# Two transformer blocks on one core: which heads of the expert router add their gates to a table and which write them plainly

## The chip, the cores and the metric

One Trainium2 chip, one of its eight cores. The kernel is one program on that core. The metric is the device time of one execution in microseconds (us); runs of one kernel are compared by their median.

## The reference

The reference applies two blocks to 512 tokens of width 1024. The first mixes latent attention, a short convolution and attention to a memory; the second has two kinds of attention with 8 heads each. Both come before the part that matters here: the feed-forward part of the second block, a retrieval from 16384 experts of one neuron each.

```
q  = (xc @ wq).reshape(chunk, 8 heads, 2 halves, 128)
s  = einsum(q, subkeys)                      # 128 scores for each half
s1, i1 = top_k(s[half 0], 16);  s2, i2 = top_k(s[half 1], 16)
cs, ci = top_k(all 256 sums s1 + s2, 16)     # 16 picks for each token and head
eidx = i1 * 128 + i2 at the picks            # number of the expert, 0 to 16383
g  = softmax(cs)
hid = xc . u_table[eidx];   a = gelu(hid) * g
out = sum over heads and picks of a * v_table[eidx]
```

Each token has 8 x 16 = 128 picks. Two heads of one token may pick the same expert; its gate is then the sum of both. Within one head the 16 picks are different experts.

## The kernel before

**Gates as a dense table.** The kernel does not gather expert rows for the first 384 tokens (three blocks of 128, `DENSE = 3`). It multiplies those tokens with all 16384 experts and weighs every product with a gate that is zero for an expert that wasn't picked. The gates stand in a table in HBM, `gates`, of 128 tiles x 128 experts x 384 tokens, set to zero earlier by the SyncE queue. The fourth block of tokens is served by gathers of rows in the output stage.

**The stages from about 1050 us on.** First the queries are projected (unit "wq", 16 of them, line 1108) and scored against the sub-keys (line 1304); ScalarE copies the results (lines 1461 and 1637); GpSimd (POOL) makes the low halves of the split weights (line 950). Then TensorE transposes the residual (line 1314) and runs the hidden stage: 128 tiles, each of 128 experts against 512 tokens in 24 matmuls (line 1325). For a tile, SyncE loads the `u` weights into one of four slots (`load_u`), ScalarE makes their high part (`high_u`, line 1643), VectorE (DVE) their low part (`low_u`, line 1954), TensorE multiplies, ScalarE applies the activation (line 1378) into one of four slots, and for tiles 0 to 95 SyncE stores the result to HBM (`keep`). The activation of a tile waits until the store of the tile four before it has landed. In the last 32 tiles the results stay on chip. The output stage (line 1336) follows.

**The retrieval on VectorE** runs in the same time. `retrieve(h)` sorts one head in eight steps; between the steps stand calls of `low_u`, 8 of them in head 2 and 12 in each later head, in an order written out by hand (`FIRST_LOWS_AT`, `LOWS_AT`). `set_gates(h - 1)` stands after the fourth of the steps that step through head h (after the first for head 0's gates) and the `low_u` calls there; head 7's gates are set after four more `low_u`. Operations on one engine that depend on each other are chained by `link`, which makes VectorE wait for its own last instruction. VectorE's code is written out until 72 tiles are split, ScalarE's until tile 68; after that they loop. TensorE and SyncE loop from the fourth tile on.

**The scatters on POOL.** One scatter writes one pick of one head for the 128 tokens of a block: 128 elements of 4 bytes at indexed places in `gates`. There are 8 heads x 3 blocks x 16 picks = 384. Ten of them (head 0, block 0) stand between the weight splits of units 10 to 14; the others follow in the order of head, block, pick. At a head's first pick POOL waits for `s_tk`, which `set_gates` raises, and at the first pick in a block for the completion of all earlier scatters of that block. Heads 0 to 3 (`PLAIN = 4`) write plainly (line 980), heads 4 to 7 use the accumulating form of the scatter (line 983), which adds to what stands in the table.

**Equal picks.** A plain write replaces what an earlier head wrote. So for heads 1 to 3 VectorE adds to each new gate the gate that an earlier head gave the same expert: it compares the 16 new picks with the 16 h earlier ones (line 2056), multiplies with the earlier gates (line 2058), takes the maximum (line 2060; the latest gate of an expert holds the whole sum and is the largest) and adds it (line 2061). That is done for each of the three blocks.

**The end of the scatters** is waited for by SyncE, before it loads the first gates for the output stage, at tile 127 of the hidden stage.

Of the kernel before, what the change touches and what calls it, by code (L numbers as in the profile page):

```python
# [26 lines left out]
ALU = mybir.AluOpType  # L27
ACT = mybir.ActivationFunctionType
AX = mybir.AxisListType

P = 128
# [15 lines left out]
TOPK = 16  # L47
NT = 128
DENSE = 3
TD = DENSE * P  # L50
PLAIN = 4
LOWS_AT = (1, 2, 1, 2, 1, 2, 1, 2)
FIRST_LOWS_AT = (0, 0, 0, 1, 2, 2, 1, 2)
EARLY = 2
# [348 lines left out]
def program(nc, t_in, out):  # L403
    build_schedule()
    ctx = ExitStack()
    with ctx:
# [20 lines left out]
        def region(off, n, k=None, of=None):  # L427
            at, base = of or ((low, 0) if off < LOW else (blocks, LOW))
            v = at[:, off - base:off - base + n]
            return v if k is None else v.rearrange("p (k n) -> p k n", k=k)  # L430
# [18 lines left out]
        expert_gate = [region(o + 2 * P * tb + P, P) for tb in range(TB)]  # L449
# [5 lines left out]
        spare_off = o  # L455
# [52 lines left out]
        def rt(off, n, k=None):  # L508
            return region(TAIL + off, n, k, (tail, TAIL))
# [7 lines left out]
        eq = rt(15360, 1024)  # L517
# [16 lines left out]
        rated = rt(19984, P)  # L534
        token = rt(20112, 4)
        sum_before = rt(20116, TOPK)
        earlier = rt(20132, DENSE * TOPK * PLAIN, DENSE)
        gf = staged[:, 0:D]
        fss = staged[:, D:D + 16]
        fsq = staged[:, 2 * D:2 * D + 8 * T].rearrange("p (u n) -> p u n", u=8)  # L540
# [138 lines left out]
        sq0, n = {}, 0  # L679
# [12 lines left out]
        auxi, n = {}, 0  # L692
# [45 lines left out]
        for n, (kind, _, loads) in enumerate(PROJ):  # L738
            if kind in SPLIT:
                same = users[kind == "br"]  # L740
# [193 lines left out]
        def _(pool):  # L934
# [36 lines left out]
            def scatter(tb, k):  # L971

                h = k // TOPK
                if tb == 0 and k % TOPK == 0:
                    pool.wait_ge(s_tk, h + 1)
                if h and k % TOPK == 0:
                    pool.wait_ge(s_sc[tb], 16 * k)
                where = bass.IndirectOffsetOnAxis(ap=expert_no[tb][:, k:k + 1], axis=0)
                if h < PLAIN:
                    nc.gpsimd.indirect_dma_start(gate_elements, where, expert_gate[tb][:, k:k + 1], None)\  # L980
                        .then_inc(s_sc[tb], 16)
                else:
                    nc.gpsimd.indirect_dma_start(gate_elements, where, expert_gate[tb][:, k:k + 1], None,  # L983
                                                 compute_op=ALU.add).then_inc(s_sc[tb], 16)
# [3 lines left out]
            for s in STEPS:  # L988
# [14 lines left out]
                elif s[0] == "mem_squares":  # L1003
                    k, mm_, total = s[1], dtmp[:, MEM:2 * MEM], dtmp[:, 0:MEM]
# [723 lines left out]
        def _(dve):  # L1728
            V = nc.vector
            chain = [0]  # L1730

            def link(ins):

                chain[0] += 1
                ins.then_inc(s_d, 1)
                dve.wait_ge(s_d, chain[0])
# [242 lines left out]
            def retrieve(h):  # L1979

                for w in range(2):
                    yield from sorted_half(2 * h + w)
                    yield
                c4 = cand.rearrange("p (t a b) -> p t a b", t=TB, a=16)
                ch = cand.rearrange("p (t n) -> p t n", t=TB)
                shape = [P, TB, 16, 16]
                link(V.tensor_tensor(c4, tva[:, :, 2 * h, :].unsqueeze(3).to_broadcast(shape),
                                     tva[:, :, 2 * h + 1, :].unsqueeze(2).to_broadcast(shape), ALU.add))
                numbers = tif.rearrange("p (t w m) -> p t w m", t=TB, w=2)
                link(V.tensor_copy(numbers, tia[:, :, 2 * h:2 * h + 2, :]))  # L1990
                for tb in range(TB):
                    ins = V.max(cs[:, tb, 0:8], ch[:, tb, :])
                link(ins)
                yield
                for tb in range(TB):
                    ins = V.max_index(ci[:, tb, 0:8], cs[:, tb, 0:8], ch[:, tb, :])
                link(ins)
                for tb in range(TB):
                    ins = V.match_replace(ch[:, tb, :], cs[:, tb, 0:8], ch[:, tb, :], -BIG)
                link(ins)  # L2000
                yield
                for tb in range(TB):
                    ins = V.max(cs[:, tb, 8:16], ch[:, tb, :])
                link(ins)
                V.tensor_tensor(ee[:, h, :].rearrange("p (t k) -> p t k", t=TB), cs,
                                cs[:, :, 0:1].to_broadcast([P, TB, 16]), ALU.subtract).then_inc(s_sm, 1)
                for tb in range(TB):
                    ins = V.max_index(ci[:, tb, 8:16], cs[:, tb, 8:16], ch[:, tb, :])
                link(ins)
                yield  # L2010
                cif = ci.rearrange("p t k -> p (t k)")
                for w in range(2):
                    if w == 0:
                        link(V.tensor_scalar(ca, cif, 4, None, ALU.logical_shift_right))
                    else:
                        link(V.tensor_scalar(ca, cif, 15, None, ALU.bitwise_and))
                    link(V.tensor_copy(cbf[:, w, :], ca))
                    q3 = eq.rearrange("p (r m) -> p r m", m=16)
                    q4 = eq.rearrange("p (t k m) -> p t k m", t=TB, k=16)
                    link(V.tensor_tensor(q3, cbf[:, w, :].unsqueeze(2).to_broadcast([P, 64, 16]),  # L2020
                                         iota16.unsqueeze(1).to_broadcast([P, 64, 16]), ALU.is_equal))
                    link(V.tensor_tensor(q4, q4, numbers[:, :, w, :].unsqueeze(2).to_broadcast(shape), ALU.mult))
                    link(V.tensor_reduce(sel[:, w, :], q3, AX.X, ALU.add))
                    if w == 0:
                        yield
                number, place = cbf[:, 0, :], cbf[:, 1, :]
                ks = slice(TOPK * h, TOPK * (h + 1))
                link(V.scalar_tensor_tensor(number, sel[:, 0, :], float(NKEYS), sel[:, 1, :], ALU.mult, ALU.add))
                for tb in range(TB):
                    part = slice(TOPK * tb, TOPK * (tb + 1))  # L2030
                    ins = V.tensor_scalar(place[:, part], number[:, part], float(TD if tb < DENSE else P),
                                          token[:, tb % DENSE:tb % DENSE + 1], ALU.mult, ALU.add)
                link(ins)
                places = place[:, 0:TOPK * DENSE].rearrange("p (t k) -> p t k", t=DENSE)
                link(V.tensor_copy(expert_lists[:, 0:DENSE, ks].bitcast(U32), places))
                if h < PLAIN:
                    link(V.tensor_copy(earlier[:, :, ks], places))
                link(V.tensor_copy(row_no[:, ks], number[:, TOPK * DENSE:]))
                link(V.tensor_copy(hidden_no[:, ks], place[:, TOPK * DENSE:]))

            def set_gates(h):

                dve.wait_ge(s_ex, h + 1)
                e3 = ee[:, h, :].rearrange("p (t k) -> p t k", t=TB)
                link(V.tensor_reduce(es[:, 0:4], e3, AX.X, ALU.add))
                link(V.reciprocal(es[:, 4:8], es[:, 0:4]))
                ks = slice(TOPK * h, TOPK * (h + 1))
                ins = V.tensor_tensor(expert_lists[:, :, P + TOPK * h:P + TOPK * (h + 1)], e3,
                                      es[:, 4:8].unsqueeze(2).to_broadcast([P, TB, 16]), ALU.mult)
                if 1 <= h < PLAIN:  # L2050
                    n = TOPK * h
                    shape = [P, TOPK, n]
                    same = eq[:, 0:TOPK * n].rearrange("p (k m) -> p k m", k=TOPK)
                    for tb in range(DENSE):
                        link(ins)
                        link(V.tensor_tensor(same, earlier[:, tb, ks].unsqueeze(2).to_broadcast(shape),  # L2056
                                             earlier[:, tb, 0:n].unsqueeze(1).to_broadcast(shape), ALU.is_equal))
                        link(V.tensor_tensor(same, same, expert_gate[tb][:, 0:n].unsqueeze(1).to_broadcast(shape),  # L2058
                                             ALU.mult))
                        link(V.tensor_reduce(sum_before, same, AX.X, ALU.max))  # L2060
                        ins = V.tensor_tensor(expert_gate[tb][:, ks], expert_gate[tb][:, ks], sum_before, ALU.add)  # L2061
                ins.then_inc(s_tk, 1)

# [14 lines left out]
            for _ in range(4):  # L2078
                low_u(lows, lows % 4)
                lows += 1  # L2080
            set_gates(PEER_HEADS - 1)
            while lows % 4:
                low_u(lows, lows % 4)
# [185 lines left out]
```

## Time and profile before

| | |
|---|---|
| median of 3 runs | 2501.72 us (2491.94 to 2502.61) |
| the profiled execution, its own time | 2497.29 us |
| its span | 2495.5 us |
| granted TensorE clock, mean over the span | 0.961 |
| TensorE matmul busy | 2294.9 us, 92% |
| VectorE busy | 1299.1 us, 52% |
| ScalarE busy | 901.5 us, 36% |
| GpSimd busy | 1163.1 us, 47% |
| plain scatters, line 980 | 192, 198.4 us busy |
| accumulating scatters, line 983 | 192, 314.8 us busy |

The span is the time between the first and the last instruction that the profiler recorded; the execution's own time is 1.8 us longer. Busy time of the matmuls is modelled and they overlap, so a full PE in a window shows best by the number of its matmuls in that window. In the rows, PE is TensorE's matmul side, PEld its weight load, DVE is VectorE, ACT ScalarE, POOL GpSimd; "a<-b" names the output and inputs, `xN` counts instructions, and the clock is a share of 2.4 GHz. The queue q1 holds what SyncE issues, q0 what GpSimd issues.

### The profile page before, as it was taken

The page shows a single profiled execution, that of the slowest core. Times are in us where ns is not written, and L with a number is a line of the kernel's source. Part 1 is how long each engine was busy: PE and PEld are TensorE (multiplying, and loading weights), DVE is VectorE, ACT ScalarE, POOL GpSimd, SP SyncE. Part 2 cuts the span into 40 slices and gives each one's busy share as a digit, 9 for nine tenths or more (in the row PEclk, how much of TensorE's full clock was granted, in tenths as well). Part 3 has the DMA queues.
Part 4 walks back from the last instruction along what each step waited for, and adds up shares of the span by engine and source line. Part 5 has one row for each costly group of instructions (what it writes and reads, how often), then busy time and mean ns, then how long its engine had stood idle before and what let it go on. Part 6 is the DMA issues. An engine that isn't in the chain of part 4 may idle for free.

```text
span 2495.5 us, 29790 instructions
## 1 busy us (share of the span) xinstructions
PE 2294.9 (92%) x9705; PEld 1779.3 (71%) x9712; DVE 1299.1 (52%) x2403; ACT 901.5 (36%) x1419; POOL 1163.1 (47%) x817
## 2 busy tenths in 40 slices
PE   7999999999999998975596599999999999999998
PEld 5666566787766766764385488888888788888887
DVE  4355433136323563874374366622222488888887
ACT  3554543336434443312121133322222333333333
POOL 3332121244432213375454658888820366555554
PEclk9999999999999999987697799999999999999999
DMA  6554233325321112211242167666643699999997
GB/s 211 190 191 135 70 90 103 95 87 186 114 76 60 43 35 84 70 58 39 64 139 88 55 147 147 144 145 145 135 108 108 228 330 341 355 349 358 355 357 249
DMA packets 208210, 392.32 MB, mean 157 GB/s; under 512 B 56160, under 2 KB 131936, under 8 KB 207872
## 3 DMA queue, kind: packets, MB, share of 16 engines
q1 hardware_dynamic: 151296, 323.89, 39.9%
q0 software_dynamic: 56832, 67.45, 10.8%
q8 instruction: 38, 0.62, 0.1%
q14 instruction: 44, 0.36, 0.0%
HBM read 330.21 MB, written 61.01 MB: 157 GB/s over the span
## 4 chain that ended last, share of the span: by engine, by line
PE 52%; issue 4%; another core or an unknown queue 3%; DVE 1%; ACT 1%; POOL 0%; DMA 0%; DVEq 0%; ACTq 0%; POOLq 0%
PE bank L1325 26%; PE bank L1336 20%; PE bank L1108 5%; PE bank L1304 1%; ACT u_tiles_split L1643 0%; POOL low L1027 0%; PE bank L1314 0%; DMA tail<-hidden_of_last_block,low 0%; DVE low L1784 0%; ACT staged L1378 0%; DVE h_low L1806 0%; DVE tail L2058 0%; DVE tail L2056 0%; DVE tail L2060 0%
## 5 line engine op out<-in xcount | busy, mean ns | idle before, releaser
L1325 PE MATMUL bank<-h_high,u_tiles_split 128*128 128x512 f32 x2048 | 643.8, 394 | 70.5 <-issue 43.9
L950 POOL TENSOR_TENSOR u_split<-blocks,u_split 128x1024 fp32r<-128x1024 f32 (+1 forms) x115 | 283.0, 2461 | 700.0 <-ACT u_split L1471 668.9
L1108 PE MATMUL bank<-h_high,u_split 128*128 128x512 f32 (+1 forms) x1712 | 567.3, 406 | 22.4 <-DVE h_low L1806 17.8
L1336 PE MATMUL bank<-v_split,a_split 128*128 128x512 f32 x2286 | 520.3, 390 | 4.6 <-DVE a_split L2096 4.6
L1325 PEld LDWEIGHTS bank<-h_high,u_tiles_split 128*128 128x128 f32 x2048 | 390.2, 191 | 162.1 <-issue 79.3
L1336 PEld LDWEIGHTS bank<-v_split,a_split 128*128 128x128 f32 x2286 | 430.1, 188 | 94.9 <-DVE v_split L2093 5.4
L1325 PE MATMUL bank<-h_low,u_tiles_split 128*128 128x512 f32 x1024 | 403.7, 394 | 14.6 <-issue 14.4
L1954 DVE TENSOR_TENSOR u_tiles_split<-tail,u_tiles_split 128x1024 fp32r<-128x1024 f32 x128 | 156.6, 1226 | 487.6 <-ACT u_tiles_split L1643 448.4
L1108 PEld LDWEIGHTS bank<-h_high,u_split 128*128 128x128 f32 (+1 forms) x1712 | 324.6, 190 | 110.9 <-issue 23.1
L983 POOL DMA_INDIRECT gates<-low x192 | 314.8, 1640 | 87.2 <-issue 58.2
L1108 PE MATMUL bank<-h_low,u_split 128*128 128x512 f32 (+1 forms) x728 | 287.9, 395 | 0.0
L1027 POOL DMA_INDIRECT low<-in_v,low x128 | 140.2, 1095 | 296.6 <-DVE low L2112 143.6
L980 POOL DMA_INDIRECT gates<-low x192 | 198.4, 1034 | 148.2 <-DVE low L2061 91.5
L1677 ACT CAST v_split<-tail 128x1024 fp32r<-128x1024 f32 x128 | 134.9, 1054 | 300.9 <-PE bank L1336 227.1
L1325 PEld LDWEIGHTS bank<-h_low,u_tiles_split 128*128 128x128 f32 x1024 | 195.4, 191 | 55.7 <-issue 15.7
L1378 ACT ACTIVATE tail<-bank 128x512 f32<-128x512 f32 x96 | 57.4, 598 | 451.3 <-PE bank L1325 223.4
L2093 DVE TENSOR_TENSOR v_split<-tail,v_split 128x1024 fp32r<-128x1024 f32 x128 | 157.0, 1227 | 69.2 <-ACT v_split L1677 56.4
L1035 POOL DMA_INDIRECT tail<-hidden_of_last_block,low x128 | 167.9, 1312 | 43.5 <-issue 38.7
L2112 DVE SCALAR_TENSOR_TENSOR low<-low,tail 128x1024 f32<-128x1024 f32 x128 | 163.8, 1279 | 1.6 <-DMA low<-in_v,low 1.3
L1108 PEld LDWEIGHTS bank<-h_low,u_split 128*128 128x128 f32 (+1 forms) x728 | 138.2, 190 | 33.0 <-issue 6.4
L1643 ACT CAST u_tiles_split<-tail 128x1024 fp32r<-128x1024 f32 x128 | 133.1, 1041 | 8.0 <-DMA tail<-in_uT 6.5
L1856 DVE TENSOR_REDUCE low<-bank 128x1 f32<-128x512 f32 (+3 forms) x112 | 59.7, 535 | 143.1 <-PE bank L1239 71.5
(201 smaller groups left out, 2474.9 us busy)
## 6 DMA issues: line engine op xcount, KB each, us to landing
tail<-in_uT SPq DMA_DIRECT2D x128, 512.0 KB
tail<-in_v SPq DMA_DIRECT2D x128, 512.0 KB
gates<-blocks SPq DMA_DIRECT2D x32, 768.0 KB, 5.8
tail<-gates SPq DMA_DIRECT2D x128, 192.0 KB
kept_hidden<-tail SPq DMA_DIRECT2D x96, 192.0 KB
tail<-kept_hidden SPq DMA_DIRECT2D x96, 192.0 KB
blocks<-in_r SPq DMA_DIRECT2D x24, 512.0 KB, 4.0
blocks<-in_conv SPq DMA_DIRECT2D x16, 512.0 KB, 4.2
```

The costliest lines, as they stand in the source:

```text
L950: nc.gpsimd.tensor_tensor(flat(u, 1)[:, 0:n], ring[:, loads[0] % NW, 0:n], flat(u, 0)[:, 0:n].bitcast(F32), ALU.subtract).then_inc(s_wlo, 1)
L980: nc.gpsimd.indirect_dma_start(gate_elements, where, expert_gate[tb][:, k:k + 1], None)\
L983: nc.gpsimd.indirect_dma_start(gate_elements, where, expert_gate[tb][:, k:k + 1], None, compute_op=ALU.add).then_inc(s_sc[tb], 16)
L1027: nc.gpsimd.indirect_dma_start(rows_in[:, k % 4, :], None, v_rows, bass.IndirectOffsetOnAxis(ap=row_no[:, k:k + 1], axis=0))\
L1035: nc.gpsimd.indirect_dma_start(picked[:, k:k + 1], None, hidden_elements, bass.IndirectOffsetOnAxis(ap=hidden_no[:, k:k + 1], axis=0))\
L1108: last = mm(ps[0:m, :], flat(u, part)[:, k * m:(k + 1) * m], x, start=(k == 0 and j == 0), stop=(k == nk - 1 and j == 2))
L1325: last = mm(bank[slot % 2][:, :], U4[:, slot, w, k, :], x[:, k, :], start=(k == 0 and x is hh and w == 0), stop=(k == KD - 1 and w == 1))
L1336: done = mm(bank[2 + 2 * tb + dh][:, :], A2[:, slot, wa, tb * P:(tb + 1) * P], V2[slot // 2][:, slot % 2, wv, dh * T:(dh + 1) * T], start= ...
L1677: nc.scalar.copy(V2[slot // 2][:, slot % 2, 0], VR[:, slot, :]).then_inc(s_vhi, 1)
L1954: V.tensor_tensor(U4[:, slot, 1].rearrange("p k e -> p (k e)"), UR[:, slot, :], U4[:, slot, 0].rearrange("p k e -> p (k e)").bitcast(F32), ...
L2093: V.tensor_tensor(V2[slot // 2][:, slot % 2, 1], VR[:, slot, :], V2[slot // 2][:, slot % 2, 0].bitcast(F32), ALU.subtract).then_inc(s_vlo, 1)
L2112: V.scalar_tensor_tensor(sparse, rows_in[:, slot, :], rated[:, bass.ds(k, 1)], sparse, ALU.mult, ALU.add).then_inc(s_axpy, 1)
```

## The change

Heads 0 to 3 (`ADDED = 4`) now use the accumulating scatter into the zeroed table; heads 4 to 7 write plainly. Heads 0 to 3 no longer look for equal picks. Heads 4 to 7 do, in two parts. Against the 64 picks of heads 0 to 3 the gates of equal picks are summed, because each of those heads holds only its own gate. From head 5 on, the picks of the earlier plainly written heads are compared as well, with the maximum as before, and the larger of the two results is added. The list of earlier picks now holds all heads and moves to another free region of SBUF. The number of scatters, their order and their waits stay as they are.

```
-PLAIN = 4
+ADDED = 4
...
-        earlier = rt(20132, DENSE * TOPK * PLAIN, DENSE)
+        most_before = rt(20132, TOPK)
+        earlier = region(spare_off, DENSE * P, DENSE)
...
-                if h < PLAIN:
+                if h >= ADDED:
                     nc.gpsimd.indirect_dma_start(gate_elements, where, expert_gate[tb][:, k:k + 1], None)\
                         .then_inc(s_sc[tb], 16)
                 else:
...
-                if h < PLAIN:
-                    link(V.tensor_copy(earlier[:, :, ks], places))
+                link(V.tensor_copy(earlier[:, :, ks], places))
...
-                if 1 <= h < PLAIN:
-                    n = TOPK * h
-                    shape = [P, TOPK, n]
-                    same = eq[:, 0:TOPK * n].rearrange("p (k m) -> p k m", k=TOPK)
+                if h >= ADDED:
+                    n = TOPK * ADDED
+
+                    def equal_picks(tb, k0, k1, result, op):
+                        shape = [P, TOPK, k1 - k0]
+                        same = eq[:, 0:TOPK * (k1 - k0)].rearrange("p (k m) -> p k m", k=TOPK)
+                        link(V.tensor_tensor(same, earlier[:, tb, ks].unsqueeze(2).to_broadcast(shape),
+                                             earlier[:, tb, k0:k1].unsqueeze(1).to_broadcast(shape), ALU.is_equal))
+                        link(V.tensor_tensor(same, same, expert_gate[tb][:, k0:k1].unsqueeze(1).to_broadcast(shape),
+                                             ALU.mult))
+                        link(V.tensor_reduce(result, same, AX.X, op))
+
                     for tb in range(DENSE):
                         link(ins)
-                        link(V.tensor_tensor(same, earlier[:, tb, ks].unsqueeze(2).to_broadcast(shape),
-                                             earlier[:, tb, 0:n].unsqueeze(1).to_broadcast(shape), ALU.is_equal))
-                        link(V.tensor_tensor(same, same, expert_gate[tb][:, 0:n].unsqueeze(1).to_broadcast(shape),
-                                             ALU.mult))
-                        link(V.tensor_reduce(sum_before, same, AX.X, ALU.max))
+                        equal_picks(tb, 0, n, sum_before, ALU.add)
+                        if h > ADDED:
+                            equal_picks(tb, n, TOPK * h, most_before, ALU.max)
+                            link(V.tensor_tensor(sum_before, sum_before, most_before, ALU.max))
                         ins = V.tensor_tensor(expert_gate[tb][:, ks], expert_gate[tb][:, ks], sum_before, ALU.add)
```

## Rows read from the trace of the kernel before

**Rows 1.** The page's slices, 40 of 62.4 us; busy share in tenths.

```profile
PE   7999999999999998975596599999999999999998
...
POOL 3332121244432213375454658888820366555554
```

**Rows 2.** Windows: length, busy us (instructions) by engine PE to POOL, clock, DMA share, GB/s.

```profile
1500.00:1550.00 50.00, 50.00 (x222) 41.40 (x222) 30.99 (x86) 14.03 (x18) 42.37 (x26) 1.00 0.69 146
1181.35:1225.60 44.25, 12.28 (x25) 6.75 (x25) 1.23 (x1) 1.53 (x2) 29.69 (x31) 0.57 0.07 18
1308.73:1336.29 27.56, 6.10 (x12) 2.90 (x13) 0.00 (x0) 0.74 (x2) 18.84 (x20) 0.59 0.04 11
1389.00:1432.22 43.22, 14.28 (x43) 9.53 (x41) 9.08 (x43) 1.53 (x2) 29.03 (x30) 0.66 0.08 20
1156.00:1957.70 801.70, 717.74 (x3072) 585.17 (x3072) 337.65 (x812) 217.71 (x280) 464.69 (x336) 0.94 0.49 118
```

**Rows 3.** Timeline of POOL: start, duration, line, operation, idle time before it.

```profile
1094.88 0.99 POOL L980 DMA_INDIRECT gates<-low  x1 [0.17 <-issue]
...
1156.95 1.69 POOL L980 DMA_INDIRECT gates<-low  x1 [14.37 <-DVE low L2061]
...
1219.23 0.95 POOL L980 DMA_INDIRECT gates<-low  x1 [0.31 <-issue]
1267.67 1.69 POOL L980 DMA_INDIRECT gates<-low  x1 [47.49 <-DVE low L2061]
...
1332.40 0.96 POOL L980 DMA_INDIRECT gates<-low  x1 [0.31 <-issue]
1362.95 1.69 POOL L980 DMA_INDIRECT gates<-low  x1 [29.59 <-DVE low L2061]
```

**Rows 4.** Lines L980 and L983: duration ns min/median/max, first and last start.

```profile
L980 POOL DMA_INDIRECT gates<-low x192: 954/958/1940, 1063.1 to 1425.9; - x192
L983 POOL DMA_INDIRECT gates<-low x192: 1552/1559/2612, 1455.9 to 1827.4; - x192
```

**Rows 5.** Waits of ACT, 1140 to 1460 us: total, times, longest.

```profile
ACT tail L1378 <- remote: 130.4, 7, 35.1
```

**Rows 6.** DMA queues: 1308 to 1334 us above the dots, 1500 to 1550 us below.

```profile
q1 hardware_dynamic: 131, 0.47, 4.7%
q0 software_dynamic: 653, 0.01, 1.9%
...
q1 hardware_dynamic: 3947, 7.26, 48.0%
q0 software_dynamic: 3689, 0.01, 21.2%
```

**Rows 7.** Timeline of PE before and at the hidden stage's start.

```profile
1120.39 2.08 PE L1304 MATMUL bank<-tail 128*128 128x128 f32 x8 [16.15 <-issue]
1149.12 5.78 PE L1314 MATMUL bank<-low 128*128 128x128 f32 x32 [26.65 <-ACT staged L1637]
1156.06 0.50 PE L1325 MATMUL bank<-h_high,u_tiles_split 128*128 128x512 f32 x1 [1.16 <-ACT low L1663]
```

**Rows 8.** Timeline of DVE at the gates of heads 1, 2 and 3.

```profile
1151.97 0.43 DVE L2056 TENSOR_TENSOR tail<-tail 128x256 f32<-128x256 f32 x1
...
1260.29 0.69 DVE L2056 TENSOR_TENSOR tail<-tail 128x512 f32<-128x512 f32 x1
...
1352.44 0.21 DVE L2045 TENSOR_REDUCE tail<-tail 128x4 f32<-128x64 f32 x1
...
1353.16 0.96 DVE L2056 TENSOR_TENSOR tail<-tail 128x768 f32<-128x768 f32 x1
...
1356.14 0.17 DVE L2061 TENSOR_TENSOR low<-low,tail 128x16 f32<-128x16 f32 x1
...
1365.55 1.22 DVE L1954 TENSOR_TENSOR u_tiles_split<-tail,u_tiles_split 128x1024 fp32r<-128x1024 f32 x1
```

**Rows 9.** Timeline of PE, the matmul after that gap.

```profile
1366.83 0.50 PE L1325 MATMUL bank<-h_high,u_tiles_split 128*128 128x512 f32 x1 [0.81 <-DVE u_tiles_split L1954]
```

## The prediction, made before the changed kernel ran

> **What bounds the kernel now.** I read the page's slices first [rows 1]. TensorE is at 9 tenths nearly everywhere. The one long dip in the second half is in slices 17 to 22 (about 1060 to 1435 us), where PE falls to 5 tenths. It is where the gate table is written with plain scatters, so I went there.
>
> The windows table gives the rate of the hidden stage. Undisturbed it is 222 matmuls in 50 us [rows 2], 4.44 per us, so one expert tile (24 matmuls) takes 5.4 us. The whole stage has 3072 matmuls in 801.7 us [rows 2]; at the full rate they take 692. So 110 us are lost inside the stage. Three of its stretches hold nearly all: 25, 12 and 43 matmuls in 44.3, 27.6 and 43.2 us [rows 2], that is 80 where 511 would fit. PE runs there at 16% of its rate and 97 us are gone. The granted clock beside them is a mean of 0.57, 0.59 and 0.66 of 2.4 GHz, so near its lower level of 1.2 GHz most of the time; the other 12 us, 4 for each, go by my estimate in the return to the upper level after each stretch.
>
> What stands beside these stretches is POOL's stream of plain scatters [rows 3]. Streams start at 1156.95, 1267.67 and 1362.95 and end near 1220.2, 1333.4 and 1426.9 (the last one by the line's own row [rows 4]); PE starves 24, 41 and 26 us after each start and is back 3 to 5 us after each end. The later accumulating scatters run in one stream from 1455.9 to 1827.4 [rows 4], 192 of them at 1.945 us each, and windows in it are full. Meanwhile ScalarE waited 130 us, 7 times, for a transfer's completion ("remote") [rows 5], though in the starved stretch the load and store queue moved only 131 packets and the scatter queue took 1.9% of the DMA engines' time; with the accumulating form it takes 21.2%, and the load and store queue moves at 48% [rows 6]. So completions are late, not bandwidth short. The Trainium skill says (DMA: Bandwidth & Descriptors, "Queues, rings and completion order") that a DMA's semaphore increment lands only after every earlier write of that engine, across its queues; by that, late completions would follow the plain stream wherever it lies, which is the forecast's side. The same section has each engine take its queues in turn, which would keep a light stream from starving another; that is the first rival's side.
>
> A fourth stream begins at 1094.88 [rows 3] with head 0. PE is at the last key projections, waits 26.65 us for ScalarE's copy and starts its transposes at 1149.12, the hidden stage at 1156.06 [rows 7].
>
> **The change part by part.** Four sums, against the profiled execution (2497.3 us; the median of the runs shown is 2501.7, and 2497.3 is within them).
>
> A. Start of the hidden stage. Head 0 is now added. The ten early scatters sit between the weight splits; the accumulating form is 0.6 us longer (1559 against 958 ns [rows 4]), two in each of five projection units, 1.2 us a unit. The first units' idle time on POOL takes part of these 6 us and PE's lead over the last split the rest; I take 0, bounds 0 and 5. The other 38 no longer starve anything: PE was free for the last key scores at 1120.39 - 16.15 = 1104.2 [rows 7], so they end near 1105. The wait for ScalarE's copy shrinks to that copy, the transposes (5.8 us) run from 1106, and 1.2 later the hidden stage begins, near 1113, not 1156.06. Late next is the low part of the second tile on VectorE, by little. Gain 43 us, bounds 0 (it starves all the same) and 50.
>
> B. The three starved stretches, heads 1 to 3, go: 110 less the 0.8 of part C, gain 109. Bounds 0 and 109.
>
> C. VectorE. The comparisons of heads 1 to 3 (256, 512 and 768 elements) go, and cost PE 0.8 us; heads 5 to 7 do the same sizes among themselves. Added on top, for heads 4 to 7 and each of 3 blocks: three operations of 1024 elements and, from head 5, a maximum. Today head 3's block runs from 1352.44, the next tile's low part starts at 1365.55 [rows 8], a gap of 13.1 us, and PE waited 0.81 for it [rows 9]; so 12.3 us are covered by the tiles split ahead. A 1024-element operation takes 1.22 us, 1.26 with its gap; 768, 512 and 256 take 0.96, 0.69 and 0.43 [rows 8], with a gap of 0.03. A small operation takes 0.21 with its gap. The 0.7 us before and 2.9 after the comparisons stay.
> Head 4: 0.7 + 3 x (3 x 1.26 + 0.21) + 2.9 = 15.6, loss 3.3. Head 5 adds 3 x (3 x 0.46 + 0.21) = 4.8, loss 8.1. Head 6 adds 7.2, loss 10.5. Head 7 adds 9.5 but nothing follows it before the next split, 22.2, loss 9.9. Sum 32 us. Bounds: 10 (heads 6 and 7 fall in time that PE starves anyway) and 65 (VectorE has only about 65 us for a head, twelve tiles, and 31 of 50 us busy [rows 2] makes 40 of 65; plus 20 it is nearly full).
>
> D. The plain scatters' new place. POOL resumes adds near 1098; 182 of them at 1.945 take 354 us, to 1452. A head's gates are set after low part 26, 38, 50, 62 and 72 for heads 3 to 7 (the code's counts), when PE is at the third tile before: 1113 + 23 x 5.4 = 1237 for head 3, and with the block and the losses of C about 1315, 1387 and 1463 for heads 4 to 6. All are ready before POOL comes to them, so the plain stream starts at 1452 and runs through three heads: 144 scatters, the first 24 at about 1.4 us and the starved rest at 1.263 (the spacing in [rows 3]), 185 us, to 1637. PE starves from 30 us after the start (the mean of the three) to 4 after the end: 159 us, at 16% of its rate, 134 lost, and 4 for the clock. PE makes some 4.6 tiles in it, from tile 64 to 69, just where head 7's gates can be set; I let head 7 run by itself afterwards, losing what a stream of one head loses now, 109 / 3 = 36. D costs 174 us. Were head 7 in time, the stream is one of 242 us, and it costs 186. Lower bound 0 (no starving there; below it nothing is to be won, since nothing starves in that place now), upper 216, if PE stands still in all of a stream of 242 less 26.
> The stores that ScalarE waits for end at tile 96, which this stream doesn't reach. POOL ends near 1740, before PE ends the stage near 2011, and the load of gates waits for nothing new.
>
> The other edits (the moved list, one more small copy for each of heads 4 to 7, 0.2 us each) are within C. The output stage after 1958 is untouched: 0.
>
> Sum: 2497.3 - 43 - 109 + 32 + 174 = 2551 us.
>
> **The rivals.**
> 1. No starving late. Mechanism: what starves is not the plain form but the early place, where engines fetch fresh code (the 16.15 us before the last key scores are "issue" [rows 7]); decided at 1482, when the stream has run 30 us. Then D is 0: 2497.3 - 43 - 109 + 32 = 2377 us, much faster. For it: ScalarE and VectorE are in their loops by tile 68 and 72. Against it: PE and SyncE are in the same loops in the second and third stretch as later, and the adds from 1455.9 run beside the same unrolled code without a loss.
> 2. The starving is not continuous: each head costs about what it costs now, 36 us, four times 145. 2497.3 - 43 - 109 + 32 + 145 = 2522. For it: only streams of one head have been seen. Against: nothing in a stream lets up with time.
> 3. VectorE becomes the bound beside a fully starved stream: C 50 and D 205, 2600 us. For it: its budget in C; a stall of it also breaks up PE's clock.
> 4. The small writes starve whatever their form, so that adds beside the projections would as well. The skill (same page, "Specifications") has transfers under 512 B done by read-modify-write in either form. The long stream of adds in [rows 4] beside full windows speaks against that. A and B would be lost: 2497 + 32 + 174 = 2703, 2%.
>
> **How the numbers follow.** Forecast 0.52, rival 1 0.20, rival 2 0.16, rival 3 0.10, rival 4 0.02. The predicted time is the forecast's, 2551. The range must reach rivals 2 and 3 and some spread of theirs: 2465 to 2620, leaving out rival 1 (0.20) and rival 4. The forecast's own range, by bounds of A, C and D about it, is 2525 to 2590. This kernel's measurement tells 0.5% (12.5 us) from nothing. Faster: rival 1 and a thin edge of rival 2, 0.22. Within 0.5%: the rest of rival 2's lower half, 0.09. Slower: 0.69.
>
> **What would show it.** A: the first hidden matmul near 1113. B: full windows from 1113 to 1430. C: PE waiting for the split line of VectorE some 3, 8 and 10 us near heads 4 to 6. D: accumulating scatters from 1098 to 1452, then plain ones, and PE's windows at a fifth of their count from 1480 to 1640, with ScalarE waiting for "remote". If those windows hold 222 matmuls per 50 us, rival 1 is right and the prediction wrong; if PE starves between 1113 and 1430, rival 4 is.

## The result, and the profile after

The changed kernel takes 2573.11 us (median of 4 runs, 2566.92 to 2581.11), the kernel before on the same chip 2496.83 us (4 runs, 2487.37 to 2502.61). The ratio is 1.0311, interval 1.0263 to 1.0359: the change makes the kernel slower by about 76 us. The forecast was 2551. The profiled execution has a span of 2573.3 us, 77.8 above the span before.

The page's slices (40 of 64.3 us; PE and POOL in tenths of busy time, the granted clock, all DMA traffic in GB/s) answer to [rows 1]:

```profile
PE   7999999999899989999998861129999999999998
...
POOL 3431122245342213688888877750000265556664
PEclk9999999999999999999999985559999999999999
...
GB/s 210 187 191 126 72 94 106 91 115 180 71 86 50 42 41 91 91 99 143 144 134 121 120 74 13 12 24 149 143 109 107 174 332 333 354 352 359 349 354 257
```

The dip before (slices 17 to 22 of [rows 1]) is gone. A deeper one has come at slices 24 to 27, about 1480 to 1735 us, with POOL busy beside it. In slices 25 to 27 the clock is at its half and few bytes are moved.

The lines of the two scatters (duration min/median/max, first and last start; L984 is the accumulating form, L981 the plain one) answer to [rows 4]:

```profile
L984 POOL DMA_INDIRECT gates<-low x192: 1552/1556/2603, 1061.4 to 1457.4; - x192
...
L981 POOL DMA_INDIRECT gates<-low x192: 966/972/1970, 1460.0 to 1714.2; - x192
```

They change places at 1459, and both streams run without a gap. The windows of the changed kernel (length, busy time and instructions of PE, PEld, DVE, ACT, POOL, then clock, DMA share, GB/s) answer to [rows 2]:

```profile
1160.00:1210.00 50.00, 50.00 (x223) 41.40 (x222) 31.68 (x76) 16.83 (x21) 42.39 (x26) 1.00 0.67 147
1310.00:1360.00 50.00, 46.77 (x200) 38.16 (x199) 42.72 (x121) 15.93 (x21) 42.54 (x25) 0.97 0.62 127
1360.00:1410.00 50.00, 42.01 (x176) 34.31 (x175) 40.18 (x87) 11.54 (x15) 42.48 (x25) 0.90 0.56 115
1484.00:1531.00 47.00, 32.38 (x130) 23.33 (x128) 14.13 (x21) 9.21 (x12) 36.62 (x35) 0.94 0.26 77
1531.00:1728.00 197.00, 38.81 (x72) 21.03 (x72) 24.87 (x30) 4.85 (x8) 141.19 (x142) 0.52 0.06 12
1735.00:2035.00 300.00, 300.00 (x1325) 248.50 (x1324) 66.20 (x54) 85.39 (x111) 0.00 (x0) 1.00 0.42 129
1109.00:2035.30 926.30, 731.70 (x3072) 589.55 (x3072) 386.90 (x872) 216.56 (x279) 494.63 (x367) 0.88 0.41 103
```

In the columns of counts the first is PE's. Beside the adds its rate is the full one, 222 in 50 us; 200 and 176 are the windows with the searches of heads 4 and 5. From 1484 the rate falls, and from 1531 to 1728, 197 us, PE makes 72 matmuls where 875 would fit. After the stream it is at once full again for 300 us. The whole stage takes 926.3 us, 124.6 more than before, and begins at 1109.0, 47.1 earlier: together 77.5 us, the whole difference of the spans.

What PE and ScalarE waited for in the starved stretch (total, times, longest), as in [rows 5]:

```profile
PE bank L1326 <- issue: 155.3, 60, 21.2
PE bank L1326 <- ACT tail L1379: 17.6, 1, 17.6
```

```profile
ACT tail L1379 <- remote: 227.0, 7, 65.6
```

Again completions that don't come ("remote"), in waits of up to 65.6 us (before, 35.1). ScalarE's timeline shows that the work goes on in steps, one tile each time that such a wait ends:

```profile
1595.94 0.60 ACT L1379 ACTIVATE tail<-bank 128x512 f32<-128x512 f32 x1 [63.67 <-remote]
...
1663.09 0.60 ACT L1379 ACTIVATE tail<-bank 128x512 f32<-128x512 f32 x1 [65.61 <-remote]
...
1727.49 0.60 ACT L1379 ACTIVATE tail<-bank 128x512 f32<-128x512 f32 x1 [62.87 <-remote]
```

What is late is the completion and not the data. By the order of the slots, the activation at 1663.09 waits for the store that was issued at 1503.7, 159 us before; the bytes of that store, and of the next tile's stores and load after it, had all moved by 1518, and from 1518 to 1531 the load and store queue moved nothing. From 1610 to 1660 us again no load or store packet was moved, because nothing was left to move: the load issued at 1606.3 was through by 1610, and SyncE's next store was issued at 1663.9. The scatter queue took 1.8%:

```profile
DMA packets 1216, 0.02 MB, mean 0 GB/s; under 512 B 1216, under 2 KB 1216, under 8 KB 1216
...
q0 software_dynamic: 1216, 0.02, 1.8%
```

PE's own row has a second part. Most of its 60 waits for "issue" (nothing that the profile shows) are not between tiles but between single matmuls: within a tile most matmuls start 2.8 us after the one before, 2.2 of it idle, where the full rate is one in 0.225. The gaps between the tiles are 21.3, 21.2 and 17.6 us. What sets the 2.8 us no run shows. It is not what bounds the stretch: the tile activated at 1663.09 had been ready in PE's bank since about 1575.

The new waits on VectorE: PE's timeline at the searches of heads 4, 5 and 6.

```profile
1319.21 0.50 PE L1326 MATMUL bank<-h_high,u_tiles_split 128*128 128x512 f32 x1 [3.23 <-DVE u_tiles_split L1955]
...
1394.42 0.80 PE L1326 MATMUL bank<-h_high,u_tiles_split 128*128 128x512 f32 x1 [7.99 <-DVE u_tiles_split L1955]
...
1472.60 0.80 PE L1326 MATMUL bank<-h_high,u_tiles_split 128*128 128x512 f32 x1 [10.43 <-DVE u_tiles_split L1955]
```

### The profile page after: what moved, and what is told of

It is laid out like the page before. It is cut to its first block, busy times and chain, and to the rows that moved or that the text cites. A ratio compares the mean times of both kernels' runs of the same rounds, so it can differ in the third digit from the quotient of the medians.

```text
span 2573.3 us, 29842 instructions
## 1 busy us (share of the span) xinstructions
PE 2304.0 (90%) x9705; PEld 1779.7 (69%) x9712; DVE 1347.4 (52%) x2455; ACT 900.9 (35%) x1419; POOL 1182.3 (46%) x817
## 3 DMA queue, kind: packets, MB, share of 16 engines
q1 hardware_dynamic: 151296, 323.89, 38.5%
## 4 chain that ended last, share of the span: by engine, by line
PE 49%; another core or an unknown queue 8%; DVE 3%; ACT 1%; issue 1%; POOL 0%; DMA 0%; DVEq 0%; ACTq 0%; POOLq 0%
PE bank L1326 24%; PE bank L1337 20%; PE bank L1109 5%; DVE tail L2058 1%; DVE tail L2056 1%; DVE tail L2060 1%; PE bank L1305 1%; ACT u_tiles_split L1644 0%; DVE u_tiles_split L1955 0%; POOL low L1028 0%; DMA tail<-hidden_of_last_block,low 0%; DVE low L1785 0%; ACT staged L1379 0%; DVE h_low L1807 0%
## 5 line engine op out<-in xcount | busy, mean ns | idle before, releaser
L1326 PE MATMUL bank<-h_high,u_tiles_split 128*128 128x512 f32 x2048 | 652.7, 398 | 162.2 <-issue 121.7
L1028 POOL DMA_INDIRECT low<-in_v,low x128 | 149.2, 1166 | 479.6 <-PE bank L1326 321.3
L984 POOL DMA_INDIRECT gates<-low x192 | 327.7, 1707 | 57.6 <-issue 57.5
L981 POOL DMA_INDIRECT gates<-low x192 | 197.0, 1026 | 58.6 <-issue 58.6
```

What stands on the lines that cost most here:

```text
L1028: nc.gpsimd.indirect_dma_start(rows_in[:, k % 4, :], None, v_rows, bass.IndirectOffsetOnAxis(ap=row_no[:, k:k + 1], axis=0))\
L1326: last = mm(bank[slot % 2][:, :], U4[:, slot, w, k, :], x[:, k, :], start=(k == 0 and x is hh and w == 0), stop=(k == KD - 1 and w == 1))
```

## The experiments

The runs fell on four chips. On the first of them the kernel before took 2497.48 us (9 runs, 2489.96 to 2510.08), about as in the measurement above (whether that was the same chip isn't known); on the three others 2347.11, 2346.60 and 2346.53 (27, 13 and 13 runs, all between 2342.32 and 2351.97). This was not looked for, and it is the main finding beside the change's own effect. Each of the four chips was used only once, at another time than the others, so "chip" here stands for the chip with all that went with that one use of it. Each comparison below is with the kernel before on the same chip.

**First chip (kernel before 2497.48 us).**

**1. All heads added.**

```
-PLAIN = 4
+PLAIN = 0
```

> All 8 heads use the accumulating scatter and no head looks for equal picks (the sum needs none). Theory (the plain form starves the other engines): the hidden stage starts near 1110, runs full for 692 us to about 1802, and the scatters, 374 at 1.945 us from about 1098, end near 1826, so the last tiles' loads wait a little for them: 2573 - (2035 - 1826) = 2364 us, at best 2340. Rival (the place starves, from 1480 us on, whatever the form): starved windows stay between 1480 and the end of the scatters, 2550 us or more. Rival (accumulating scatters starve too when they stand first): no, since the changed kernel had full windows beside them from 1110 to 1310.

Measured: 2366.46 us (5 runs), ratio 0.9468, interval 0.9435 to 0.9500. The windows table of the whole hidden stage and the waits at its end:

```profile
1300.00:1350.00 50.00, 50.00 (x222) 41.42 (x221) 33.92 (x96) 16.63 (x21) 42.38 (x26) 1.00 0.67 144
1111.70:1808.00 696.30, 696.28 (x3072) 576.50 (x3072) 319.33 (x780) 216.43 (x279) 587.74 (x357) 1.00 0.66 136
```

```profile
PE bank L1335 <- DVE a_split L2093: 24.1, 1, 24.1
```

The stage takes 696.3 us, with no starvation anywhere, at a late place and beside unrolled code alike. The wait of 24.1 us at the change of stage is for the gates, whose last scatter starts at 1823.0. The place alone starves nothing, and the changed kernel starves in a late place: the rival that gave 2377 for the change is out.

**2. Plain scatters, slower.**

```
                 if h < PLAIN:
                     ...  # the plain scatter
+                    nc.gpsimd.memset(region(spare_off, 600), 0.0).then_inc(s_pace, 1)
+                    pace[0] += 1
+                    pool.wait_ge(s_pace, pace[0])
```

> The kernel before, with a 600-column fill of an unused region on POOL (and a wait for it) after each plain scatter, so that plain scatters come about every 1.9 us instead of 1.26, the spacing of the accumulating ones. Theory pace (completions starve because writes come too fast): no starved window, the hidden stage starts near 1113 and loses nothing: about 2497 - 152 = 2345, with the scatters' end near 1830 holding it up to 2365. Theory form (a plain scatter starves at any pace): a starved stretch becomes longer with the stream (48 x 1.9 = 91 us a head), about 60 us lost for each of heads 1 to 3 and for the start: 2560 us or more.

Measured: 2366.02 us (4 runs), ratio 0.9469, interval 0.9432 to 0.9507. The form is the same, 192 scatters of 964 ns (median); only the 0.61 us fill and its wait stand between them, so one starts 1.9 us after the other:

```profile
1200.63 1.02 POOL L982 DMA_INDIRECT gates<-low  x1 [0.28 <-POOL low L984]
1201.66 0.61 POOL L984 MEMSET low<- 128x600 f32 x1
1202.55 0.96 POOL L982 DMA_INDIRECT gates<-low  x1 [0.28 <-POOL low L984]
```

```profile
1300.00:1350.00 50.00, 50.00 (x222) 41.41 (x222) 35.20 (x94) 16.84 (x21) 42.95 (x52) 1.00 0.49 148
...
1108.20:1807.30 699.10, 696.83 (x3071) 576.55 (x3072) 346.01 (x817) 216.87 (x279) 592.74 (x534) 1.00 0.56 135
```

Full windows. So on this chip the plain form doesn't starve by itself; it does when one comes every 1.26 us, and not when one comes every 1.9 with POOL's fill and wait between (the pace and the pause were not tried apart).

**3. No search for equal picks.**

```
-                if h >= ADDED:
-                    ...  # the search and the sum
```

> The changed kernel without the comparison with earlier picks on any head, so a gate of an expert picked twice is wrong; the scatters stay as they are. The search costs TensorE what the trace shows as waits for VectorE near heads 4 to 6 (3.2, 8.0 and 10.4 us): the hidden stage is 22 us ahead when the plain stream begins, at the same time as before, so 2573 - 22 = 2551 us. If VectorE were a bound beyond these waits, 2530 or less. If the search is hidden, 2573.

Measured: 2566.87 us (4 runs, 2558.46 to 2567.41), ratio to the kernel before 1.0271, interval 1.0231 to 1.0311. That is 6 us less than the changed kernel's median, which was measured at another time, where 22 less were expected; the intervals of the two ratios overlap (1.0263 to 1.0359 for the changed kernel), so the 6 us are not clear of noise. The two profiled executions differ by 16.7. The trace shows where the rest of the gain went: PE comes to the stream further on, but the stream starts 9 us earlier (1450.9, where 1460.0 was the changed kernel's) and PE starves sooner. PE's windows around the stream, and what POOL waited for in it:

```profile
1440.00:1490.00 50.00, 33.80 (x136) 26.50 (x135) 20.33 (x44) 10.49 (x13) 39.03 (x37) 0.84 0.34 82
1490.00:1540.00 50.00, 7.04 (x12) 3.44 (x12) 0.00 (x0) 0.00 (x0) 38.11 (x40) 0.50 0.02 1
...
1590.00:1640.00 50.00, 9.34 (x18) 5.26 (x18) 1.23 (x1) 1.53 (x2) 35.41 (x36) 0.53 0.07 16
1640.00:1690.00 50.00, 35.12 (x125) 26.41 (x126) 6.66 (x8) 7.68 (x10) 21.71 (x22) 0.77 0.26 79
1690.00:1740.00 50.00, 22.62 (x61) 14.63 (x60) 4.20 (x4) 6.24 (x8) 25.81 (x27) 0.57 0.18 51
1740.00:1790.00 50.00, 50.00 (x222) 41.43 (x221) 11.73 (x10) 13.80 (x18) 0.00 (x0) 1.00 0.48 144
1108.70:2020.40 911.70, 732.70 (x3072) 589.82 (x3072) 319.17 (x780) 217.10 (x279) 478.32 (x366) 0.87 0.43 104
```

```profile
POOL gates L981 <- DVE low L2047: 25.8, 1, 25.8
```

PE has 12 matmuls from 1490 to 1540, where the changed kernel still had 130 from 1484 to 1531. So the low parts that head 7's gates stand behind came late, POOL waited 25.8 us for them and took up its stream at 1661.9, and head 7 then starved PE by itself. This is the course that the prediction had for the changed kernel. The price of the search under starvation isn't settled by this pair; experiments 7 and 8 measure it without starvation.

**4. Neighbouring places.**

```
-                    ins = V.tensor_scalar(place[:, part], number[:, part], float(TD if tb < DENSE else P),
+                    ins = V.tensor_scalar(place[:, part], number[:, part] if tb == DENSE else iota[:, ks],
+                                          float(TD if tb < DENSE else P),
```

> The kernel before, but the places of the dense blocks' gates come from the number of the pick and not from the expert: the 128 elements of one scatter lie side by side (512 bytes of one table row) instead of in 128 rows; the gates are wrong, the number, form, size and order of scatters are the same. If spread single-element writes in memory are what starves the others, the starved windows go: 2345 to 2365 us. If it is the scatter's form or pace whatever the addresses, 2497 us.

With this edit each scatter writes within one row of the table, and all scatters together within the rows of its first tile; the run doesn't tell these two kinds of crowding apart. Measured: 2676.64 us (4 runs), ratio 1.0712, interval 1.067 to 1.0755. Neither theory's number. The plain streams still starve the others ("remote"), and a second cost is there that the accumulating form has as well: PE's window beside it isn't full (143 matmuls in 50 us from 1550 to 1600), and ScalarE waits for the weights' loads, 304.6 of its 359.8 us between 1480 and 1880. ScalarE's waits, 1100 to 2100 us:

```profile
ACT u_tiles_split L1643 <- DMA tail<-in_uT: 359.8, 54, 15.1
...
ACT tail L1378 <- remote: 90.9, 4, 50.9
```

So the starvation does not need the 128 writes to be spread over 128 rows, and crowding them costs more than it saves.

**Second chip (kernel before 2347.11 us).** The next four kernels were made to find the limit of the pace. On this chip there was nothing to find it by.

**5 and 6. Shorter fills, 200 and 100 columns** in the diff of experiment 2.

> The kernel before with a 200-column fill after each plain scatter: about 1.5 us from one to the next (85 writes of 4 bytes per us; plain now 101, starving; accumulating 66, and plain behind the 600-column fill 67, both harmless). If the limit lies above 85 per us: no starvation, and the scatters end about 80 us earlier than with the long fill, so the wait of 24 us at the change of stage goes too: 2366 - 24 = 2342 us. If it lies below, completions pile up more slowly than now, a part of the starvation stays: 2380 to 2480 us.

> The same with a 100-column fill: about 1.4 us, 91 writes per us. Limit above 91: 2342 us. Between 85 and 91: more than the 200-column kernel, 2400 us or more. If it is not a matter of pace but of whether POOL does anything else between two scatters, both fills give the same as the long one but end earlier, 2342 us.

Measured: 2347.19 us (11 runs), ratio 1.0004, interval 0.9995 to 1.0014; and 2345.47 us (10 runs), 0.9995, interval 0.9983 to 1.0007. The first expectation's 2342 is nearly met, but the kernel before has the same time here, so this tells nothing of the limit. Both were run once more on other chips:

> The kernel before with the 100-column fill (one plain scatter in about 1.38 us, 93 writes per us). Beside a kernel before of 2497 us: if the limit lies above that pace 2345, if below, a part of the starvation: 2380 to 2490. Beside 2347: 2347 again, which tells nothing of the limit.

> The kernel before with the 200-column fill (one plain scatter in about 1.5 us). Beside a kernel before of 2497 us: 2345 if the limit of pace lies above 85 writes per us, 2380 to 2480 if below it. Beside 2347: 2347 again.

Measured: 2344.90 beside 2346.60 (ratio 0.9996, interval 0.9985 to 1.0007), and 2347.95 beside 2346.53 (1.0002, 0.9989 to 1.0015). Again chips without starvation. What the repeats do show is that the fills cost nothing there: POOL has the time.

**7. The changed kernel, plain scatters with the long fill.** The diff of experiment 2 in the changed kernel, for `h >= ADDED` (the fill stands in another unused region).

> The changed kernel with the 600-column fill after each plain scatter (now heads 4 to 7). Theory pace: nothing starves in the late place either; what is left of the change is the search on VectorE, now for all four heads at full speed, 3.2 + 8.0 + 10.4 + 10 = 32 us: hidden stage 1109 + 692 + 32 = 1833 us, past the scatters' end near 1823, so 2573 - (2035 - 1833) = 2371 us. If the late place had a cost of its own: 2420 us or more.

Measured: 2385.58 us (4 runs), ratio 1.0171, interval 1.0155 to 1.0187, that is 38.5 us above the kernel before on this chip. This is the price of the search, with nothing starving. The expected 2371 was 14.6 too low. The hidden stage takes 737.2 us where 724 were worked out. PE's four waits for VectorE are 31.9, as foreseen; but without any starvation or such waits the stage takes not 692 us but 696.3 (experiment 1), and about 9 us are lost beside the waits. The granted clock falls there: it is a mean of 0.90 in the window with head 5's wait in the changed kernel of the result.

**Half the elements in a plain scatter** (`expert_no[tb][0:64, k:k + 1]` and the gates likewise).

> The kernel before, but a plain scatter writes only 64 of the 128 tokens of its block (the other tokens' gates of heads 0 to 3 are left out). Number of scatters and of semaphore increments as before. If the number of written elements per us starves (64 in at most 1.26 us is 51 per us or, should a scatter take half the time, up to 100): with the instruction as long as before no starvation, 2342 to 2350 us; if it becomes half as long, 2450 or more. If scatters or their increments per us do it: 2497 us or more.

Measured: 2348.91 us (10 runs), ratio 1.0013, interval 1.0003 to 1.0023. Inconclusive for the same reason. It shows one thing: a scatter of 64 elements takes POOL 892 ns (median), one of 128 takes 958 (median, kernel before), so POOL's time for one hardly depends on the number of elements.

**Third chip (kernel before 2346.60 us). 8. The changed kernel once more.**

> The changed kernel as it is. On two chips the kernel before took 2497 and 2347 us. Theory: the starvation by plain scatters at full pace belongs to the chip as well; where the kernel before takes 2347, nothing starves in the changed one either, and what is left is the search on VectorE (32 to 38 us): 2380 to 2386 us. Where the kernel before takes 2497, it repeats 2573. Rival: the long late stream starves on every chip: 2450 us or more beside 2347.

Measured: 2382.25 us (4 runs, 2380.59 to 2385.76), ratio 1.0161, interval 1.0144 to 1.0177. The long plain stream is there as before, 192 scatters from 1458.6 to 1722.5, one every 1.38 us (1.33 in the changed kernel of the result), and nothing starves:

```profile
1500.00:1550.00 50.00, 39.92 (x165) 32.46 (x164) 29.61 (x34) 9.61 (x14) 39.02 (x37) 0.86 0.38 111
1550.00:1600.00 50.00, 50.00 (x222) 41.44 (x221) 11.03 (x9) 14.84 (x20) 38.73 (x38) 1.00 0.46 142
1600.00:1650.00 50.00, 50.00 (x222) 41.40 (x222) 11.62 (x10) 14.22 (x19) 38.89 (x37) 1.00 0.48 146
1650.00:1700.00 50.00, 50.00 (x222) 41.41 (x221) 11.67 (x10) 13.80 (x18) 38.86 (x37) 1.00 0.45 129
```

```profile
PE bank L1326 <- DVE u_tiles_split L1955: 31.7, 4, 10.4
```

```profile
q1 hardware_dynamic: 3888, 7.08, 45.5%
q0 software_dynamic: 1152, 0.02, 1.7%
```

From 1550 on the windows beside the stream are full, loads and stores move at 45.5% beside a scatter queue of 1.7% (1610 to 1660 us), and ScalarE has no "remote" wait. The change costs 35.7 us here, nearly all of it in the four waits for VectorE, 31.7 us.

**Fourth chip (kernel before 2346.53 us). 9. Neighbouring places once more.**

> The kernel before with the 128 elements of a scatter side by side; the gates are wrong. On the chip whose kernel before took 2497 it took 2677, with loads of weights slowed beside both forms. Beside a kernel before of 2347 us: if writes crowded on few places of memory are a limit of every chip, 2500 us or more here too; if both slowdowns belong to that chip, 2347.

Measured: 2604.49 us (4 runs), ratio 1.1102, interval 1.1063 to 1.1140. So that cost belongs to no one chip. ScalarE waits 521 us for loads, and never for "remote":

```profile
ACT u_tiles_split L1643 <- DMA tail<-in_uT: 521.4, 80, 15.1
```

Here the plain form has this cost too:

```profile
1350.00:1400.00 50.00, 35.05 (x121) 27.05 (x120) 16.81 (x51) 9.09 (x11) 35.50 (x35) 0.83 0.96 79
```

The DMA engines are busy in it for 96% of the time and move 79 GB/s; in a full window of the kernel before it is 69% and 146 [rows 2]. In the starved stretch of the result they were busy for 6%. So the two costs are different things: crowded places keep the DMA engines busy and delay the data, on both chips tried; the plain stream at full pace delays completions beside idle DMA engines, on the first chip. On the second and fourth chip the plain stream ran at full pace only in kernels that were timed and not traced (the kernel before) or had other scatters; that it starves nothing there is read from their time.

## Why the prediction was right or wrong

The direction, the place and the mechanism were right for the chip on which it was made and measured; the size was short, 54 us forecast and 76 measured. That the sum came so near is in part luck: A and C erred by 4 us each to the change's favour, D by 32 against it.

**A, the start.** Right. The hidden stage begins at 1109.0; 1113 was forecast, 47 us won where 43 were. The early adds cost PE nothing that can be seen.

**B, the three early stretches.** Right. From 1110 to 1310 the windows hold 222 or 223.

**C, the search.** The mechanism and the single waits are right: 3.23, 8.0 and 10.43 us where 3.3, 8.1 and 10.5 were worked out. Head 7's search fell into the starved stretch here, as its lower bound allowed. Without starvation (experiment 8) the four waits make 31.7, with 32 forecast; the kernel loses 35.7 (and 38.5 in experiment 7). The term left out is what comes after such waits: in the window of the last one, 1500 to 1550 us, the clock is 0.86. In the changed kernel of the result the three windows with the waits (1310 to 1410 and 1460 to 1484 us) lack 28 us of matmuls where the waits are 21.7, so C cost 28 there, by three searches and not by four.

**D, the late stream.** The term of the sum that was mis-sized: 174 us forecast. What the stage lost is 926.3 - 692 = 234, less C's 28: 206 (4 of them are lost without any starvation, since the undisturbed stage takes 696.3 in experiment 1). The rate in the starved time was nearly right as a mean, 202 matmuls of 1083 from 1484 to 1728, 19% where 16% was taken (it is 130 in the first 47 us and 8% of the full rate after them). The length was not: 244 us starved, where the forecast had 159 and, for head 7 by itself, about 38 (the mean of the three stretches before), 197 together.

About 19 of the missing 47 us come from the sentence "I let head 7 run by itself afterwards". PE came far enough in the first 47 us for head 7's search to end at 1620.8, before POOL was through with head 6 at 1653.7, so the stream had no break. For a stream without a break the forecast's own alternative has 242 - 26 = 216 us starved, at a cost of 186. The other 28 us are missing in that alternative as well. The stream lasted 255 us and not 242 (by the forecast's own spacings, 24 of 1.4 us and then 1.263, 192 scatters take 246, a slip in its working; measured are 1.28 in the starved part). PE starved from 24 us after its start, where 30 was taken. And it was back 14 us after the last scatter's start at 1714.2, where 4 was taken, because it had to wait for the next completion in ScalarE's steps of 64 to 67 us.

The measured 206 lies between the alternative's 186 and the bound of 216. Experiment 3 shows the other course, with the break, at 219.7 us lost in its stage (911.7 less 692), so the break would not have saved what the forecast let it save.

**The rivals.** Rival 2, a fixed 36 us for each head, is out: 206 / 4 = 52. "Nothing in a stream lets up", the argument against it, isn't quite so: one tile gets through about every 65 us. Rival 1 (the early place starves, 2377 us) is refuted by the changed kernel and by experiment 1. Rival 3 had the starvation right (205) and the search too high (50); its mechanism, VectorE as the bound, isn't seen, since VectorE itself waited for ScalarE in that time (186.4 us of its waits from 1484 to 1735). Rival 4 (small writes in either form) is refuted on the first chip by the adds at 1110.

**What the prediction took for granted** was that the starvation is the kernel's. It needs plain scatters at about 1.26 us each and a chip that has it. The rule on late semaphore increments that it leaned on (the Trainium skill, DMA: Bandwidth & Descriptors, "Queues, rings and completion order") agrees with the "remote" waits on the first chip as far as they go: the data had moved and the completion was late. But which earlier writes an increment would have waited for there, no run shows, and the same stream delays none on the third chip. The rule of the same section that engines take their queues in turn isn't contradicted on the first chip, as the prediction would have it: the load issued at 1606.3 had moved its 0.52 MB by 1610, beside the stream.

On the third chip the changed kernel was 1.6% slower by C alone, D costing nothing. On the second, with the long fill, it was 1.7% slower; on the fourth it was not run. That the gains of A and B don't exist on those three chips follows from the time of the kernel before, which is 150 us shorter there, about what A and B are worth on the first (47 and 110); no trace of that kernel was taken on them.

**Open.** What differs between the chips was not tried and can't be told from these traces, nor whether it is the chip at all or something else that differed between the four uses, such as where the tables lay in memory. Also open is why PE issues its matmuls 2.8 us apart in the starved stretch. Nor is it known where the limit of pace lies on the first chip, between 67 writes per us (128 in 1.92 us, harmless) and 101 (128 in 1.263, starving); nor whether the number of writes or of scatters counts there, nor whether a pause of POOL between two of them matters by itself beside the pace that it sets. Experiments 5, 6 and that with half the elements would have told, had they met that chip.

**Towards a version for both.** On the first chip all heads added and the long fill give 2366 us, 131 less than before. On the others the kernel before is already at 2347, and the fill of 100 or 200 columns keeps that. Whether the short fill is enough on the first chip is the open point above; neither the long fill in the kernel before nor all heads added was timed on the others, so no version is shown to be good on both.

## What to carry to other kernels

When an engine starves beside almost idle DMA queues, look at which stream of small writes runs beside it and slow that stream down before moving it: moving took the loss along and joined four short ones into one long one. How long a stream of transfers will be depends on the engines that it starves, so work out both courses, with and without a break; and take the end of a starved stretch from how the work gets through it, here in steps of 65 us, and not from shorter stretches. Look at whether the data or only the completion is late: the time at which the bytes moved tells it. And a saving that rests on a starvation should be measured on more than one chip, since here three of four didn't have it.

## What was not expected of the hardware

- The same kernel takes 2497 us on one chip and 2347 on three others, steadily in each (9 and 53 runs), each chip in one use. On the first, starvation by a stream of 4-byte scatters of 128 elements every 1.26 us accounts for the 150 us (47 and 110 by the trace). In that state ScalarE waited 61 to 66 us at a time for completions of stores whose data had long moved; one came 159 us after the store was issued.
- Putting the 128 elements of each scatter side by side, in one row of the table and not in 128, and all scatters into one tile of it, makes the kernel 7 and 11% slower on two chips: the traffic of loads and stores beside it falls from about 146 to about 90 GB/s, with the DMA engines busy for 93% of the time and more.
- POOL takes 0.96 us for a plain scatter of 128 elements, 0.89 for one of 64, and 1.56 for the accumulating one of 128.
